# A column of ones beside the values, and one product per bank for the last tile of keys, in the mLSTM heads of a hybrid encoder step

## What is computed

```python
s = jnp.einsum('bthk,bshk->bhts', qf, kf) * w_intra
num = jnp.einsum('bhts,bshv->bthv', s, vf) + jnp.einsum('bht,bthk,bhkv->bthv', w_inter, qf, C0)
den = jnp.sum(s, axis=-1) + w_inter * jnp.einsum('bthk,bhk->bht', qf, n0)
...
C_new = decay[..., None, None] * C0 + jnp.einsum('bhs,bshk,bshv->bhkv', w_end, kf, vf)
n_new = decay[..., None] * n0 + jnp.einsum('bhs,bshk->bhk', w_end, kf)
```

## Time and profile before

| | |
|---|---|
| median of 3 executions | 1975.74 us (1975.45 to 1983.57) |
| the profiled execution, its own time | 1974.71 us |
| span in its trace | 1973.0 us |
| PE, matmuls busy | 1860.3 us (94%) |
| DVE busy | 1235.8 us (63%) |
| ACT busy | 1000.7 us (51%) |
| POOL busy | 107.1 us (5%) |
| mean granted TensorE clock | 0.98 of full |

### The profile page before, as it was taken

One profiled execution on the slowest core, in us unless ns is written; L12 is line 12 of the kernel. 1 busy time (PEld: TensorE's weight loads), 2 busy tenths in 40 slices (PEclk: granted clock), 3 DMA queues, 4 the chain that ended last, 5 costly groups with the idle time before them and its releaser, 6 DMA issues.

```text
span 1973.0 us, 28043 instructions
## 1 busy us (share of the span) xinstructions
PE 1860.3 (94%) x11679; PEld 1669.4 (85%) x11679; DVE 1235.8 (63%) x1421; ACT 1000.7 (51%) x991; POOL 107.1 (5%) x188
## 2 busy tenths in 40 slices
PE   7999999999999999999999999999889988998981
PEld 6999999999999999999999999998666665666650
DVE  5764553556555555563433355444799999999984
ACT  5334654653434433453234233333678787878761
POOL 3001001000000000000000000000100000000001
PEclk9999999999999999999999999998999999999995
DMA  7664554545554455445555666446699999999975
GB/s 202 161 161 128 151 143 129 145 129 139 134 143 133 129 139 148 131 134 152 161 159 151 188 182 172 129 128 243 252 373 425 408 414 399 421 412 397 414 308 159
DMA packets 381501, 425.32 MB, mean 216 GB/s; under 512 B 14095, under 2 KB 361083, under 8 KB 365305
## 3 DMA queue, kind: packets, MB, share of 16 engines
q1 hardware_dynamic: 372185, 388.07, 60.2%
q0 software_dynamic: 7504, 29.75, 4.2%
q10 hardware_dynamic: 1712, 6.04, 1.0%
HBM read 408.36 MB, written 15.47 MB: 215 GB/s over the span
## 4 chain that ended last, share of the span: by engine, by line
PE 78%; DMA 9%; DVE 7%; issue 3%; ACT 2%; SPq 0%; DVEq 0%; POOL 0%; POOLq 0%; ACTq 0%
PE bank L645 17%; PE bank L647 17%; PE bank L646 16%; DMA ring<-in_w_exp_gate 4%; DMA ring<-in_w_exp_down 4%; PE bank L947 3%; PE bank L949 3%; PE bank L948 3%; PE bank L703 3%; DVE w_low L1802 2%; PE bank L805 2%; PE bank L807 2%; PE bank L806 2%; ACT w_high L1252 2%; PE bank L753 1%
## 5 line engine op out<-in xcount | busy, mean ns | idle before, releaser
L1390 DVE TENSOR_TENSOR low<-ring,high 128x2048 fp32r<-128x2048 f32 x172 | 394.1, 2291 | 575.6 <-ACT high L1028 575.4
L645 PE MATMUL bank<-x_high,high 128*128 128x304 f32 x2160 | 662.6, 307 | 0.0
L647 PE MATMUL bank<-x_high,low 128*128 128x304 f32 x2160 | 652.0, 302 | 0.0
L1028 ACT ACTIVATE high<-ring 128x2048 fp32r<-128x2048 f32 x172 | 329.1, 1913 | 542.4 <-DMA ring<-in_w_in 328.7
L646 PE MATMUL bank<-x_low,high 128*128 128x304 f32 x1904 | 572.2, 301 | 0.0
L1802 DVE TENSOR_TENSOR w_low<-ring,w_high 128x2048 fp32r<-128x2048 f32 x192 | 430.4, 2284 | 19.6 <-ACT w_high L1252 18.4
L1252 ACT ACTIVATE w_high<-ring 128x2048 fp32r<-128x2048 f32 x192 | 363.3, 1920 | 91.9 <-DMA ring<-in_w_exp_gate 35.0
L645 PEld LDWEIGHTS bank<-x_high,high 128*128 128x128 f32 x2160 | 405.9, 188 | 2.2
L647 PEld LDWEIGHTS bank<-x_high,low 128*128 128x128 f32 x2160 | 406.0, 188 | 0.0
L646 PEld LDWEIGHTS bank<-x_low,high 128*128 128x128 f32 x1904 | 358.5, 188 | 1.4
L920 PE MATMUL bank<-w_high,xs 128*128 128x512 f32 x512 | 212.2, 414 | 28.8 <-DVE xs L1813 13.1
(11 more groups left out here) (367 smaller groups left out, 2107.5 us busy)
## 6 DMA issues: line engine op xcount, KB each, us to landing
ring<-in_w_in SPq DMA_DIRECT2D x120, 1024.0 KB, 5.6
ring<-in_w_exp_gate SPq DMA_DIRECT2D x32, 2048.0 KB, 8.7
ring<-in_w_exp_up SPq DMA_DIRECT2D x32, 2048.0 KB, 10.4
ring<-in_w_exp_down SPq DMA_DIRECT2D x32, 2048.0 KB, 10.3
ring<-in_w_proj_rnn SPq DMA_DIRECT2D x20, 1024.0 KB, 6.0
ring<-in_w_proj_mlstm SPq DMA_DIRECT2D x16, 1024.0 KB, 6.0
ring<-in_w_out SPq DMA_DIRECT2D x16, 1024.0 KB, 6.0
slot_out<-HB POOLq DMA_DIRECT2D x16, 512.0 KB, 8.4
```

Source lines behind the costliest of these rows:

```text
L645: pe.matmul(dst, hi[:, k, :], rhs_high(k), start=(k == 0), stop=False)
L647: last = pe.matmul(dst, lo[:, k, :], rhs_high(k), start=False, stop=(k == KD - 1))
L1028: act.activation(high[n % 4], raw[n % 4], ACT.Copy).then_inc(t_split, 1)
L1390: v.tensor_tensor(low[n % 4], raw[n % 4], high[n % 4].bitcast(F32), ALU.subtract).then_inc(t_rest, 1)
```

## The change

Three things are changed. The values of a head get a 257th column that holds ones (`VW` = 257), written once by a memset at product 55; `states` then takes four matmuls of 257 columns, and the normaliser is the last column of their result. In `dw` and in bank 4 the second tile of keys starts at column 304 and no longer at 272, and columns 272 to 303 of `dw` are set to zero once; the first matmul of each bank in `numerators` then covers all 304 columns, and the last tile of keys is one matmul of 48 columns. Since the first tile no longer touches the second in `dw`, DVE multiplies them in two instructions. The row `BW` of a head in `HB` grows from 1376 to 1379 words, and `dw` by 32.

```diff
-        BW = 2 * T + 3 * DV
+        VW = DV + 1
+        BW = 2 * T + 3 * VW
...
-        SC = [(P, 0, TP, 0), (P, TP, TP - P, P), (NL, TP + TP - P, NL, 2 * P)]
+        SC = [(P, 0, TP, 0), (P, T, TP - P, P), (NL, T + TP - P, NL, 2 * P)]
...
-                    pe.matmul(bank[b][:, 0:TP], left(0, P), dw[:, 0:TP], start=True, stop=False)
-                    pe.matmul(bank[b][:, P:TP], left(1, P), dw[:, TP:TP + TP - P], start=False, stop=False)
+                    pe.matmul(bank[b][:, 0:T], left(0, P), dw[:, 0:T], start=True, stop=False)
+                    pe.matmul(bank[b][:, P:TP], left(1, P), dw[:, T:T + TP - P], start=False, stop=False)
                     c = SC[2][1]
-                    pe.matmul(bank[b][:, 2 * P:TP], left(2, NL), dw[0:NL, c:c + PL], start=False, stop=False)
-                    pe.matmul(bank[b][:, TP:T], left(2, NL), dw[0:NL, c + PL:c + NL], start=False, stop=False)
+                    pe.matmul(bank[b][:, 2 * P:T], left(2, NL), dw[0:NL, c:c + NL], start=False, stop=False)
...
-                for c in range(2):
-                    dst = bank[6][:, 0:DV] if c == 0 else bank[7][:, 0:1]
-                    for i, (t, n) in enumerate(TT):
-                        r_ = HB[0:n, h, HV0 + i * DV:HV0 + (i + 1) * DV] if c == 0 else ones[0:n, 0:1]
-                        pe.matmul(dst, kp[0:n, i * DQK:(i + 1) * DQK], r_, start=(i == 0), stop=(i == 2))
-                    dst = bank[6][:, DV:2 * DV] if c == 0 else bank[7][:, 1:2]
-                    r_ = HB[0:NL, h, HV0 + 2 * DV:HV0 + 3 * DV] if c == 0 else ones[0:NL, 0:1]
-                    last = pe.matmul(dst, ks[0:NL, :], r_, start=True, stop=True)
-                last.then_inc(pe_cn, 1)
+                for i, (t, n) in enumerate(TT):
+                    pe.matmul(bank[6][:, 0:VW], kp[0:n, i * DQK:(i + 1) * DQK], HB[0:n, h, HV0 + i * VW:HV0 + (i + 1) * VW],
+                              start=(i == 0), stop=(i == 2))
+                pe.matmul(bank[7][:, 0:VW], ks[0:NL, :], HB[0:NL, h, HV0 + 2 * VW:HV0 + 3 * VW], start=True, stop=True).then_inc(pe_cn, 1)
...
+                v.memset(dw[:, TP:T], 0.0)
                 v.tensor_copy(hb16[:, :], bank[7][:, 0:2 * NH]).then_inc(gt_ready, 1)
...
-                v.tensor_tensor(dw[:, 0:c], dw[:, 0:c], bank[4][:, 0:c], ALU.mult)
+                v.tensor_tensor(dw[:, 0:TP], dw[:, 0:TP], bank[4][:, 0:TP], ALU.mult)
+                v.tensor_tensor(dw[:, T:c], dw[:, T:c], bank[4][:, T:c], ALU.mult)
                 v.tensor_tensor(dw[0:NL, c:c + NL], dw[0:NL, c:c + NL], bank[4][0:NL, c:c + NL], ALU.mult).then_inc(sw_ready, 1)
...
+                if n == N_GIF:
+                    v.memset(HB[:, :, HV0:BW].rearrange("p h (a n) -> p h a n", a=3)[:, :, :, DV:VW], 1.0)
```

More of the change, by code:

```diff
@@ L167, in build @@
         og_s = ml(2 * T)
-        DW = T + TP - P - NS + NL
+        DW = T + TP - P + NL
         dw, hh, sq = ml(DW), ml(2 * T), ml(2 * T)
@@ L726, in left @@
                     def left(i, n):
-                        return ones[0:n, :] if lt is None else HB[0:n, h, HV0 + i * DV + lt * P:HV0 + i * DV + (lt + 1) * P]
-                    pe.matmul(bank[b][:, 0:TP], left(0, P), dw[:, 0:TP], start=True, stop=False)
-                    pe.matmul(bank[b][:, P:TP], left(1, P), dw[:, TP:TP + TP - P], start=False, stop=False)
+                        return ones[0:n, :] if lt is None else HB[0:n, h, HV0 + i * VW + lt * P:HV0 + i * VW + (lt + 1) * P]
+                    pe.matmul(bank[b][:, 0:T], left(0, P), dw[:, 0:T], start=True, stop=False)
+                    pe.matmul(bank[b][:, P:TP], left(1, P), dw[:, T:T + TP - P], start=False, stop=False)
                     c = SC[2][1]
-                    pe.matmul(bank[b][:, 2 * P:TP], left(2, NL), dw[0:NL, c:c + PL], start=False, stop=False)
-                    pe.matmul(bank[b][:, TP:T], left(2, NL), dw[0:NL, c + PL:c + NL], start=False, stop=False)
+                    pe.matmul(bank[b][:, 2 * P:T], left(2, NL), dw[0:NL, c:c + NL], start=False, stop=False)
                     l0 = n0b if lt is None else c0[:, lt * P:(lt + 1) * P]
@@ L1508, in values_in @@
                 h, c = INDEX[t] // 2, INDEX[t] % 2
-                dst = HB[:, h, HV0:HV0 + 3 * DV].rearrange("p (a n) -> p a n", a=3)[:, :, c * P:(c + 1) * P]
+                dst = HB[:, h, HV0:HV0 + 3 * VW].rearrange("p (a n) -> p a n", a=3)[:, :, c * P:(c + 1) * P]
                 v.tensor_copy(dst[:, 0:2, :], bank[t % 4][:, 0:2 * P].rearrange("p (a n) -> p a n", a=2))
@@ L1515, in state_out @@
                 v.tensor_copy(cn[:, 0:DV], bank[6][:, 0:DV])
-                v.tensor_copy(nst[:, h:h + 1], bank[7][:, 0:1])
+                v.tensor_copy(nst[:, h:h + 1], bank[6][:, DV:VW])
                 v.scalar_tensor_tensor(out=nst[:, h + NH:h + NH + 1], in0=vec[:, V_N0 + h:V_N0 + h + 1], scalar=hb16[:, h:h + 1],
-                                       in1=bank[7][:, 1:2], op0=ALU.mult, op1=ALU.add)
-                v.scalar_tensor_tensor(out=cn[:, DV:2 * DV], in0=c0, scalar=hb16[:, h:h + 1], in1=bank[6][:, DV:2 * DV],
+                                       in1=bank[7][:, DV:VW], op0=ALU.mult, op1=ALU.add)
+                v.scalar_tensor_tensor(out=cn[:, DV:2 * DV], in0=c0, scalar=hb16[:, h:h + 1], in1=bank[7][:, 0:DV],
                                        op0=ALU.mult, op1=ALU.add).then_inc(cn_ready, 1)
@@ L1530, in decay_weights @@
                 v.tensor_tensor(dw[:, 0:TP], nm[:, 0:TP], tri[:, 0:TP], ALU.add)
-                v.tensor_tensor(dw[:, TP:2 * TP - P], nm[:, P:TP], tri[:, 0:TP - P], ALU.add)
+                v.tensor_tensor(dw[:, T:T + TP - P], nm[:, P:TP], tri[:, 0:TP - P], ALU.add)
                 c = SC[2][1]
```

## The result

The changed kernel takes 1967.47 us, the median of 6 executions (1962.81 to 1969.97); the kernel before, run beside it, 1977.76 us (1975.45 to 1983.57). The ratio is 0.9943 with a 95% interval of 0.9928 to 0.9958: 11.3 us faster, between 8.3 and 14.2. Forecast were 12.7 us and 1963.0 us, with a range of 1960 to 1969. Two of the 4.5 us between 1963.0 and 1967.47 are in the median of the kernel before, which was 1975.74 for the three runs shown ahead of the forecast and is 1977.76 over six.

What follows compares the result with a forecast made beforehand. PE, never idle in the heads, was taken as the bound there; 8.5 us from states plus 4.2 from numerators made 12.7 us, 1975.74 down to 1963.0, range 1960 to 1969.

Steps and rivals of the forecast that it cites:

- the sum as worked out: Whole kernel: 8.5 us from states plus 4.2 from numerators, 12.7 us less, 1960.3 to 1965.7 us; chance 0.72.
- (b): Rival: experts' stretch or a new wait in the heads returns 3 to 12 us of the gain, about 1970 us; chance 0.12.
- (c): Rival: small passes hide each other less; a head saves 0.8, a bank 0.12, 9.3 us in all, 1966.4; chance 0.08.
- the term of the numerators: Numerators: one pair of passes fewer, a wider first matmul; 0.175 us a bank, 4.2 us over 24 banks.
- PE bounds the stretch: Heads' stretch: PE is never idle there, so what it is spared comes off the time and the later part moves forward.
- States, 1.06 us a head: States: the passes with ones take 1.07 us, the 257th column adds 0.01; 1.06 us saved a head, 8.5 us in eight.
- A lone small matmul's 25 ns: States: by the skill page's figure 64 passes would be 1.6 us, not 8.5; the forecast went by the trace's 0.13 us.
- what goes with the pair: Numerators: removing one pair of passes in a bank saves 0.22 to 0.24 us, taken as 0.23.
- the 48 columns were not free: Numerators: the remaining pair's 48 columns were forecast to be free, though three times as many as in L731.
- the bound of 3.9: Numerators: lower bound of the saving over 24 banks, 3.9 to 4.4 us around 4.2.
- DVE's extra multiply: DVE in each head: multiply of 416 columns becomes 272 and 144, 0.06 us more, fits the 0.5 us slack in head 1.
- Rival (a), odd words,: L646 with hb_rounded: 256 fp32r matmuls starting at odd words lose pace, at worst 30 us, time 1993; chance 0.08.

Runs made afterwards that it cites:

- the two halves: The kernel before with only the column of ones and four states matmuls (ratio 0.9958), and with only the new dw layout and merged numerators matmul (0.9973).
- the full rows: The changed kernel with the last tile of keys on 128 rows, zeros behind row 48, in numerators and states; ratio to the kernel before 0.9877.
- the half with the states: The kernel before with only the column of ones and the four matmuls of states, dw and numerators as before; ratio 0.9958, 8.3 us.
- the even rows: The changed kernel with one unused word more in each row of HB, 1380 in place of 1379; ratio to the kernel before 0.9942.
- the run with the wide sets: The kernel before with two added sets of eight passes a head in states, 128 columns wide, result not used; ratio 1.0173.
- full rows alone: The kernel before, without the change, with the last tile of keys on 128 rows in numerators and states; ratio 0.9941.
- both runs: The kernel before with states' eight one-column passes issued three times (ratio 1.0191), and with 16 one-column passes added on one 128-row left operand (1.0163).

## Why the prediction was right, point by point

**The number, and how much of it is luck.** What PE was spared was forecast as 12.7 us and is 12.2 in the trace. The time is another matter: 1967.47 us lies in the range given, 1960 to 1969, but above the 1960.3 to 1965.7 that the forecast gave for the sum as worked out. It falls where the range had been widened for rivals (b) and (c), and neither of them is what happened. Of the 4.5 us that it is too high, 2.0 are in the kernel before, 0.5 in the term of the numerators, and the remaining 2 are within the spread of the executions. That the time stayed in the range is partly luck. The changed kernel measured once more was 13.5 us below before.

**PE bounds the stretch, and what it is spared comes off the time.** Shown: the two halves took 8.4 and 3.8 us off the heads, and their ratios, 8.3 and 5.3 us, hold these numbers; the full rows took 10.8 more off the heads and, against the changed kernel run beside them (0.9932 and 0.9877), 11 off the time. The precision is that of the ratios, some 3 us.

**States, 1.06 us a head.** Measured 1.06 (3.08 to 2.02). The 257th column costs nothing that can be seen. A lone small matmul's 25 ns, which the Trainium skill's page TensorE: Matmul & The Clock Gate gives (Back-to-back issue gap), would have made the half with the states an estimated 1.6 us; its ratio says 8.3, between 5.7 and 10.9.

**Numerators, 0.175 us a bank.** Measured 0.156 (0.467 a head). The term that was too large is what goes with the pair, 0.21 us and not 0.23. The two passes that went had taken 0.11 each. But the 48 columns were not free, as the forecast had them: the first pass of the merged pair takes 0.147 us from start to start, where the first pass of L731 with its 16 columns took 0.133. On full rows the same two passes take 0.043 and 0.029, again 0.014 apart. The pair that stays so takes 0.35 us. The wider L729 costs 0.05 more, as forecast. In all it is 3.7 and not 4.2 us, below the bound of 3.9 that I gave, which makes 12.2 in place of 12.7.

**DVE's extra multiply.** It costs nothing. Head 1 on the timeline of DVE, against the earlier trace rows,

```profile
556.15 0.44 DVE L1534 TENSOR_TENSOR XG<-XG,bank 128x272 f32<-128x272 f32 x1 [0.68 <-ACT XG L1098]
556.50 0.30 DVE L1535 TENSOR_TENSOR XG<-XG,bank 128x144 f32<-128x144 f32 x1
556.72 0.19 DVE L1536 TENSOR_TENSOR XG<-XG,bank 48x48 f32<-48x48 f32 x1
```

and of PE, against the earlier trace rows:

```profile
558.43 0.30 PE L648 MATMUL bank<-x_high,low 128*128 128x304 f32 x1
558.57 0.67 PE L729 MATMUL bank<-XG,ones 128*128 128x304 f32 x2
```

The two multiplies take 0.57 us from start to start instead of 0.51, and the chain ends 1.66 us ahead of PE, not 0.5: how early it ends goes with when the load of weights lands, which moves by more than a microsecond between executions.

**Rival (a), odd words,** is refuted by the row of `hb_rounded` and by the even rows. The forecast says that in heads 1, 3, 5 and 7 every operand in `HB` starts at an odd word; that is so for the slices of `hb_rounded`, but the tiles of values are 257 words apart, so the second tile starts at an even word in those heads and at an odd one in the others. Both kinds are in every head of the states, which take 2.02 or 2.03 us in all of them. **Rival (b), given back behind PE,** is not seen as an effect of the change: the executions of one kernel differ by up to 12 us (19 in the run with the wide sets and in that with full rows alone), and the traces of the experts' stretch by up to 10, in kernels with the change and without. **Rival (c)** is refuted for the states, which gave back all of their 1.06 us. In the numerators a bank saved 0.156 us, between the 0.175 of the sum and the 0.12 of the rival, and most of the difference is the longer first pass of the merged pair.

What stays open: why the experts' stretch differs by up to 10 us between executions when the routing and the gather have no long half-clock stretch, and what separates the runs of passes that bring the clock down from those that don't, since passes of 128 columns did it in three heads of eight.

## What to carry to other kernels

Where TensorE is the bound, price a small fp32 matmul by its distance to the next start (here 0.11 us a pass between passes on as many rows, two passes a matmul, from 1 to 128 columns) and move its work into a column or a few rows of a wider one; a column of ones beside the values gives a sum for the price of one column. A left operand of fewer rows is not cheaper but dearer where its neighbours have 128: pad it with zero rows, which brought as much again as the change, for a few memsets. And when matmuls are added or removed as a test, look at the granted clock before believing the total.

## What the runs showed of the hardware that I had not expected

- The granted clock falls to half for 3.4 us with PE busy throughout, behind some 3 us of passes of one column, with or without changes of rows (in all eight heads of both runs, in three of eight behind the wide sets). Each such stretch costs about 1.5 us.
- Going from 128 rows of the left operand to 48 and back costs the stream 0.32 us in a bank of the numerators, 0.38 in six passes of the gather. Passes within the block of 48 rows take the 0.11 us of those on 128. A pair of 48 columns took 0.35 us on 48 rows and 0.16 on 128.
- fp32r reads at an odd word run at the same pace: 302 ns in both rows, 139.7 and 139.8 ns from start to start, over 480 matmuls.
